# A retention head's output projection: the first tile pair issued by halves around the samples' small matmuls, and transposes that no longer wait for the evicted gate tiles

## The reference, cut to what matters

```python
def _ret_mixer(x, w_in, gn_g, gn_b, w_out, s0, pos0):
    h = x @ w_in
    q, k, v, g = jnp.split(h, ...)
    q = _rotary(...)
    k = _rotary(...) * (DK_C ** -0.5)
    o, S = _retention(q, k, v, s0)
    y = (jax.nn.silu(g) * _head_norm(o, gn_g, gn_b)) @ w_out
    return y, S
```

## Time and profile before

| | |
|---|---|
| median of 3 runs | 1901.61 us (1901.48 to 1903.22) |
| the profiled execution: its own time | 1901.31 us |
| its span, first to last instruction | 1899.5 us |
| TensorE busy | 93% of the span |
| VectorE, ScalarE, GpSimd busy | 47%, 28%, 8% |
| mean granted TensorE clock | 0.967 of full |
| the four heads, with their inputs and outputs | about 857 to 1453 us of the span |

### The profile page before, as it was taken

The page is one execution under the profiler, slowest core; times in us unless marked ns, Lnnn a source line. Parts: engine busy times, 40 slices in busy tenths (PEclk is TensorE's granted clock), DMA queues, the critical chain, the costliest instruction groups (busy, mean ns, idle before and its releaser), DMA issues.

```text
span 1899.5 us, 35060 instructions
## 1 busy us (share of the span) xinstructions
PE 1769.9 (93%) x13474; PEld 1593.2 (84%) x13474; DVE 893.0 (47%) x1435; ACT 528.6 (28%) x742; POOL 151.2 (8%) x137
## 2 busy tenths in 40 slices
PE   8999897879999999979989989989987999999996
PEld 8766565779999999969669859949947999999995
DVE  3344455556552455352362263254256655245543
ACT  3324333233221222142222222322223322122213
POOL 0000002001000000004013013012110100000000
PEclk9999998899999999999989989989998999999998
DMA  8888785112222223212342333333423223222221
GB/s 284 290 283 284 263 290 185 34 56 78 88 94 83 79 87 101 87 45 89 107 144 99 118 134 109 129 121 103 147 88 99 71 88 105 79 81 88 89 92 47
DMA packets 84222, 234.65 MB, mean 124 GB/s; under 512 B 9778, under 2 KB 10067, under 8 KB 83779
## 3 DMA queue, kind: packets, MB, share of 16 engines
q1 hardware_dynamic: 80834, 218.97, 34.1%
q0 software_dynamic: 3328, 14.92, 2.2%
HBM read 210.05 MB, written 23.80 MB: 123 GB/s over the span
## 4 chain that ended last, share of the span: by engine, by line
PE 64%; issue 24%; DVE 6%; DMA 3%; ACT 3%; POOL 1%; SPq 0%; DVEq 0%; ACTq 0%; POOLq 0%
PE banks L1267 50%; PE banks L1612 2%; PE banks L1604 1%; PE banks L1532 1%; PE banks L1294 1%; PE banks L1369 1%; PE banks L1382 1%; PE banks L1592 1%; DMA s<-in_s 1%; DMA kv<-in_vc 1%; PE banks L1330 1%; PE banks L1621 1%; POOL y L417 1%; PE banks L1372 1%; DMA out_ret_s<-s 1%
## 5 line engine op out<-in xcount | busy, mean ns | idle before, releaser
L1267 PE MATMUL banks<-x_hi,w_hi 128*128 128x272 f32 x2624 | 552.4, 292 | 33.5 <-DVE x_lo L1034 22.5
L1267 PE MATMUL banks<-x_hi,w_lo 128*128 128x272 f32 x2624 | 547.2, 290 | 0.0
L1267 PE MATMUL banks<-x_lo,w_hi 128*128 128x272 f32 x2624 | 545.4, 290 | 0.0
L694 DVE TENSOR_TENSOR w_lo<-w_raw,w_hi 128x1024 fp32r<-128x1024 f32 (+2 forms) x228 | 284.9, 1250 | 523.8 <-ACT w_hi L462 523.7
L462 ACT ACTIVATE w_hi<-w_raw 128x1024 fp32r<-128x1024 f32 (+2 forms) x228 | 238.2, 1045 | 943.7 <-PE banks L1267 921.7
L1267 PEld LDWEIGHTS banks<-x_hi,w_hi 128*128 128x128 f32 x2624 | 416.4, 190 | 52.5 <-issue 35.7
L1267 PEld LDWEIGHTS banks<-x_lo,w_hi 128*128 128x128 f32 x2624 | 416.9, 191 | 0.0
L1267 PEld LDWEIGHTS banks<-x_hi,w_lo 128*128 128x128 f32 x2624 | 413.9, 191 | 0.0
L1267 PE MATMUL banks<-act_lo,w_hi 128*128 128x272 f32 x704 | 145.3, 287 | 0.0
L1267 PE MATMUL banks<-act_hi,w_hi 128*128 128x272 f32 x704 | 145.1, 287 | 0.0
L1267 PE MATMUL banks<-act_hi,w_lo 128*128 128x272 f32 x704 | 145.1, 287 | 0.0
(11 more groups left out here) (232 smaller groups left out, 1703.7 us busy)
## 6 DMA issues: line engine op xcount, KB each, us to landing
w_raw<-in_w_up SPq DMA_DIRECT2D x88, 512.0 KB, 3.3
kv<-in_kc SPq DMA_DIRECT2D x128, 256.0 KB, 4.6
kv<-in_vc SPq DMA_DIRECT2D x128, 256.0 KB, 4.3
w_raw<-in_w_rin SPq DMA_DIRECT2D x48, 512.0 KB, 3.2
w_raw<-in_w_dn SPq DMA_DIRECT2D x32, 704.0 KB, 4.1
s<-in_s SPq DMA_DIRECT2D x32, 512.0 KB, 7.4
out_ret_s<-s SPq DMA_DIRECT2D x32, 512.0 KB, 2.8
w_raw<-in_w_in_ab POOLq DMA_DIRECT2D x16, 512.0 KB, 5.3
```

The lines of the kernel that those rows point to most:

```text
L694: V.tensor_tensor(w_lo[:, j, 0:k * P], w_raw[:, j, 0:k * P], w_hi[:, j, 0:k * P].bitcast(F32), ALU.subtract).then_inc(lo_ready, 1)
L1267: last = mm(B[:, 2 * j + half, 0:HN], a[:, j, w], x[:, kt, half * HN:(half + 1) * HN], start=kt == 0 and n == 0, stop=kt == k - 1 and n == 2)
```

## The change

The wait for the last two gate tiles' evictions moves from before the transposes to behind them, ahead of the scores, which write banks 0 to 3. The first output tile pair is taken out of the loop and written as four pieces of 12 matmuls each, one bank each: (tile 0, half 0), the samples' four small matmuls, (tile 1, half 0), the wait for `mlo_ready` 5, (tile 0, half 1), (tile 1, half 1). The first piece waits for `mlo_ready` 1, 2, 3 and 4, each ahead of the feature block that needs it. The loop runs over the remaining three pairs. Nothing changes on the other engines or in SyncE's queue.

```diff
                 pe.wait_ge(roped, h * 4 + 4)
-                for j in range(2):
-                    pe.wait_ge(evicted[j], h * (N_RET // 2) + (U_RET // 2 + N_RIN // 2 + 1))
...
                     last.then_inc(rv_done, 1)
 
+                for j in range(2):
+                    pe.wait_ge(evicted[j], h * (N_RET // 2) + (U_RET // 2 + N_RIN // 2 + 1))
                 for j in range(NB):
...
-                    if b == 7:
-                        pe.wait_ge(rnorm, h * 5 + 5)
-                        apart(pe)
-                        for et in range(4):
-                            last = mm(B[:, 3, et * TS:(et + 1) * TS], onat[:, NB, et * P:(et + 1) * P], stack[:, :],
-                                      start=True, stop=True)
-                        last.then_inc(rb_done, 1)
+
+                def sample_columns():
+                    pe.wait_ge(rnorm, h * 5 + 5)
+                    apart(pe)
+                    for et in range(4):
+                        last = mm(B[:, 3, et * TS:(et + 1) * TS], onat[:, NB, et * P:(et + 1) * P], stack[:, :],
+                                  start=True, stop=True)
+                    last.then_inc(rb_done, 1)
+
+                def out_half(j, half):
+                    u = U_RET + N_RIN + j
+                    if half == 0:
+                        pe.wait_ge(lo_ready, h * N_RET + (u + 1))
+                        pe.wait_ge(evicted[j], h * (N_RET // 2) + (u // 2 + 1))
+                    for kt in range(4):
+                        if half == 0 and j == 0:
+                            pe.wait_ge(mlo_ready, h * 5 + (kt + 1))
+                        w = slice(kt * P, (kt + 1) * P)
+                        for n, (a, x) in enumerate(((w_hi, m_hi), (w_hi, m_lo), (w_lo, m_hi))):
+                            last = mm(B[:, 2 * j + half, 0:HN], a[:, j, w], x[:, kt, half * HN:(half + 1) * HN],
+                                      start=kt == 0 and n == 0, stop=kt == 3 and n == 2)
+                    if half:
+                        last.then_inc(tile_done, 1)
+
+                out_half(0, 0)
+                sample_columns()
+                out_half(1, 0)
                 pe.wait_ge(mlo_ready, h * 5 + 5)
                 apart(pe)
-                with pe.Fori(0, N_OUT // 2) as i:
+                out_half(0, 1)
+                out_half(1, 1)
+                with pe.Fori(1, N_OUT // 2) as i:
```

## The result

The changed kernel takes 1906.6 us in the median of 7 runs (1902.4 to 1909.0), the kernel before beside it 1897.7 (1896.5 to 1903.2): a ratio of **1.0041** (95% interval 1.0026 to 1.0056), slower by 7.8 us by that ratio; the two medians differ by 8.9. The profiled execution took 1904.26 us, its span 1902.4. Two single executions among the experiments, of 3483 and 9123 us, are left out of their ratios.

A forecast was written before the change was run, and what follows sets the result against it. TensorE, busy for 93% of the span, bounds the kernel, leaving its pauses and half-clock stretches to win. Transposes 0, tile 2's start +4.0 and clock +6.4 gave +10.4 us on 1901.31; forecast 1911.5, range 1903 to 1916.

The forecast's parts named there:

- Part A: Transposes in each head: running the first ones during the 1.38 us eviction wait gains 0, covered by ScalarE's table load.
- The delay of `gate_samples`: VectorE in head 0: fourth `m_lo` block ends at 969.91, `gate_samples` starts at 972.77, 2.0 us later than before.
- The chain from there to tile 2: From `gate_samples` over states, store and weight load to tile 2: 10.56 us in head 0, 9.46 with landing 3.3.
- The later start of tile 2: Output tile 2 starts later by 2.0, 0.7, 0.2 or 0.3, and 1.0 us in heads 0 to 3, together +4.0.
- The new pause and the clock: TensorE pauses before tile 2, then runs at half clock: 1.6 us lost a head, +6.4 us in all.
- The wait rows: TensorE's wait for `w_lo` rises from 2.5 us to some 15, once a head before tile 2.
- The wait without the clock: Rival: pauses before tile 2 stay short or resume at full clock; +1.4 to +5.2 us, about 1905.5; chance 0.18.
- The faster one: Rival: tile 2's weights are there in time, so the halves' gain stays; -11 to -13 us, or 1890; chance 0.08.

The follow-up runs named there:

- the filled pause: Changed kernel plus 26 unread matmuls in the pause before tile 2 of each head: ratio 1.0004 to the kernel before, stretch 524.9 us.
- three ways: Changed kernel with tile 2 and 3 loads before the last stores (0.9990), both states before `gate_samples` (0.9982), or loads behind state(6)'s store (0.9967).

## Why the prediction was right, point by point

The forecast was +10.4 us and 1911.5. The stretch gave +10.6, and the median 8.9 us more than the one beside it, 7.8 by the ratio. It was slower, as forecast, and by the mechanism forecast. The forecast of the time itself is 4.9 too high; 3.9 of that is the kernel before, which I took at its first three executions, 1901.6, and which was 1897.7 beside the changed one. That the stretch agrees to 0.2 us is luck, with profiles of one kernel scattering by 2 or 3.

- **Part A, 0.** Right: 1.0003 alone. The step's reason, that the pause moves behind the first transposes, stands in the rows. I named the v copies only and forecast a wait of about 1.7 for them; it is 0.66, and VectorE's copy of k takes the other 0.80.
- **The delay of `gate_samples`.** Forecast 2.86 us after the fourth `m_lo` block ends in head 0, measured 963.67 - 960.91 = 2.76. Moving the small matmuls alone took it back to 0.88.
- **The chain from there to tile 2.** Forecast 9.46 with a landing of 3.3, measured 973.04 - 963.67 = 9.37, with a landing of 3.2. One term of head 0's was of one execution only: the landing of 4.40 in the earlier trace rows was 3.2 after the change, and 3.3 in the second profile of the kernel before. Head 0 is not special, and my +2.0 for it was about 1.1 too high against an execution without that landing.
- **The later start of tile 2.** Forecast 4.0 in all, measured 4.2, but not head by head: forecast 2.0, 0.7, 0.25 and 1.0, measured 0.8, 0.3, 2.3 and 0.9. Between the two profiles of the unchanged kernel the same parts differ by as much (-1.0, -1.4, +2.2, +0.4), so the single heads prove nothing, and the good sum owes something to luck: the terms of heads 0, 1 and 3 were too high by about as much as head 2's was too low.
- **The new pause and the clock.** Forecast a pause of 4.4 in head 0 and up to 3.8 in head 1, and 1.6 us of lost clock a head. The pause was 3.3 to 3.5 in all four. Behind the start of tile 2 the heads took 1.5 to 1.7 us longer each, 6.4 together, which is the forecast's term. In the eleven profiles without an unfilled pause of over 3 us ahead of tile 2 this part took 326.3 to 327.2 us, in the two with one 332.9 and 333.2. The largest term of the sum rested on the fewest rows and came out best. Its picture was a little off: in heads 1 and 3 tile 2 did not start at half clock, it fell to it 0.8 us later.
- **The wait rows.** Forecast "some 15" for `w_lo`, measured 15.3.

The rivals. The wait without the clock (1905.5) lies nearer the measured median than my 1911.5, but only since the kernel before was faster than I took it; the windows at tile 2 and the filled pause rule its mechanism out. The faster one, -11 to -13 with the weights there in time, was right in what it asked for: issue the load about 4 us sooner. With that done, three ways, the gain over the kernel before was 3 to 5 us of stretch and 2 to 6 of time, not 11. One thing I had left out is what is late next: tile 0 is now finished only 12 matmuls ahead of tile 2, and VectorE's eviction, sum and subtraction behind it last 0.8 us longer than those, 3 us in all. Another is that the full clock did not come early enough: with the loads behind the store of state(6), TensorE was busy for 486.8 us of the stretch with as many matmuls as it did in 483.5 before. That these two make up the whole difference is an estimate, 5.2 + 3 + 3.3 = 11.5; no run takes them apart.

What remains open: how much the sooner small matmuls are worth once the loads are early. Between those two kernels the stretch fell by 6.7 us, the median by 2.6, and I had forecast 2. The two intervals of the ratio, 0.9929 to 0.9965 and 0.9952 to 0.9982, overlap a little. The profile has two heads at a clock that the others rarely reach, and no run separates that from the edit.

## What to carry to other kernels

A wait that the profile shows on the busiest engine is worth removing only as far as the next thing is there in time: before moving work ahead of a step, follow what hangs on that step on the other engines and, above all, what stands behind it in a DMA queue. Here small matmuls put 2 us later delayed two merges, a store, and the weight loads behind that store. A pause that opens anew can also cost the clock: after 3.1 to 3.7 us of standing still ahead of tile 2 there came some 3.4 us at half speed, in all eight heads with such a pause, and after 1.3 to 2.1 there was none. The same halves, with the loads moved ahead of the last stores and the small matmuls kept early, turn 0.4% slower into 0.5% faster.

## What the runs showed of the hardware that was not expected

- More matmuls made the changed kernel faster: 104 added ones took 7.3 us off the heads, 6.9 of it behind the start of tile 2, where the half clock had cost 6.4.
- The same head of the same kernel differs by up to 2 us between executions, with its mean granted clock (head 2 of the kernel before: 150.1 us at 0.97 and 152.1 at 0.94). A forecast of a few us on one profile can't be finer than that.
- One weight load, the first behind the stores in head 0, took 4.40 us to land in the first profile of before and 3.3 in the second. A term read from a single row may be of one execution. The other first loads of the two kernels, before and after, took 3.1 to 3.5. DMA: Bandwidth & Descriptors in the Trainium skill (Anatomy of one DMA) has a fit for DMAs that GpSimd issues, 2.0 us plus the bytes at 436 GB/s. SyncE issues these loads, so the estimate of 2.6 for their 256 KB, in the prediction too, takes that fit beyond what the section covers. No first load behind a store was that quick here; in the profile of before, the later loads of the output tiles took 2.5 to 2.8.
